# A second row added at the end of its own slot, sample heads picked two ahead, token rows in two buffers: an expert mixer beside dense steps

## Chip, cores and metric

One core of a Trainium2 chip. The time is that of one launch on the device in microseconds; lower is better. The median of three runs counts.

## What is computed

One layer of a streaming encoder for 1024 prompt tokens and 64 sample tokens: a dense part (input projection, three attention branches, gates, output projection), then for each token a mixture of single-neuron experts. Cut to the part that the change touches:

```python
def one_block(xb):                                   # 128 tokens, 8 heads
    q = (xb @ w_q).reshape(blk, PEER_HEADS, 2, PEER_DHALF)
    s = jnp.einsum('thpc,hpkc->thpk', q, sub_keys)
    s1, i1 = lax.top_k(s[:, :, 0], PEER_TOPK)        # 16 of 128 on each side
    s2, i2 = lax.top_k(s[:, :, 1], PEER_TOPK)
    ...
    top, pos = lax.top_k(cand, PEER_TOPK)            # 16 of the 256 sums
    idx = jnp.take_along_axis(cidx, pos, axis=-1)
    g = jax.nn.softmax(top, axis=-1)
    u = jnp.take(u_tab, idx, axis=0)
    a = jax.nn.gelu(jnp.einsum('thkd,td->thk', u, xb), approximate=False)
    w = (g * a).astype(xb.dtype)
    return jnp.einsum('thk,thkd->td', w, jnp.take(v_tab, idx, axis=0))
```

Every token fetches 8 x 16 rows of u and v by its own numbers: 128 tokens of a tile fetch one row of 8 KB (u and v side by side) in one gather.

## The kernel before

**Tiles and groups.** The tokens are 9 tiles (8 of 128, and the sample tile of 64). They form four groups: tile 0; 1 and 2; 3 to 5; 6 to 8. While the expert work of a group runs, the dense steps of the next group run beside it. The dense steps of a group are preparation and input projection (in_prep, in_unit), attention (mix, fox, past), gates (gate), output projection (out) and the scores of the experts (sco).

**Pairs and slots.** The expert work of a head is cut into pairs of two expert ranks: 8 pairs a head, 4 in the sample tile, where two halves of 64 partitions share a gather. `make_plan` lays out one slot for each pair and spreads the dense steps over the slots of a group by their given costs, so that they are done 16 slots before the group's end. The last 16 slots of each of the first three groups, and all 160 slots of the last group, have no dense step. Every engine walks through this plan in the same order (`walk`, L657), each with its own part. VectorE, ScalarE and GpSimd take the pair first and the dense steps of the slot after it; TensorE and SP take the dense steps first.

**A pair.** GpSimd issues two indirect gathers into a ring of 8 rows, that is 4 pairs (`gather`, L1798, the issue on L1814), three pairs ahead. VectorE multiplies the u half of each row with the token rows `h_cur` and sums (`dot`, L1726, the instruction on L1733). ScalarE waits for that, takes the Gelu (L1414), multiplies it with the softmax weight (L1417) and writes the weight onto a diagonal (L1422). TensorE multiplies the diagonal with the v half into the sum `p_y` (L1250).

**The second row.** In tiles 0 to 5 TensorE takes only the first row of a pair. The second is added by VectorE (`values`, L1738, the instruction on L1749): weight times v half plus `ysb`. VectorE does this for pair n-1 behind the dot products of pair n. It waits for `s_diag` (ScalarE has made the weights) and raises `s_vapart`. GpSimd gathers pair n only when TensorE is done with pair n-4 (`s_vdone`) and, in these tiles, VectorE has added its second row.

**The pick.** VectorE finds the 16 experts of a head in four pieces (`pick`, L1762): best of each side; best sums, first and second half; expert numbers and softmax weights. It does the pieces for head n+1 in the slots q = 0 to 3 of head n, behind dot products and addition. `softmax_weights` (L1713) writes numbers and weights into one of two buffers. In a prompt head the last four slots have no piece. In a sample head all four slots have one, and the numbers are ready at the head's end. ScalarE's exponentials for it (`soften`, L1403) stand behind the weights of q = 2.

**The token rows.** `h_cur` is one buffer. SP waits for the last dot product of tile i and then loads the rows of tile i+1 (`load_h`, L903, issued on L906, called from L926 ff.). The scores of head n+2 are loaded at the first slot of head n (`load_sc`, L896), behind the store of the tile before where a tile begins.

```python
        def pair(i, r, q):                       # VectorE, L1780
            dot(i, r, q)
            values(pair_index(i, r, q) - 1)
            if r == 0 and q == 0 and i:
                finish(i - 1)
            pick(i * HEADS + r + 1, q)
```

Of the kernel before, what the change touches and what calls it, by code (L numbers as in the profile page):

```python
# [71 lines left out]
def pairs_of(i):  # L72
    return 8 if i < TILES else 4
# [15 lines left out]

ALL_PAIRS = [(i, r, q) for i in range(NT) for r in range(HEADS) for q in range(pairs_of(i))]  # L90
ALL_HEADS = [(i, r) for i in range(NT) for r in range(HEADS)]


def weight_items():
# [369 lines left out]
def layer(nc, c, t_in, outs, dram, ctx):  # L464
# [76 lines left out]


    ring = c.ring
    h_cur = sb("h_cur", [128, D])
    diag = sb("diag", [128, RING, 128])
    sc = [sb(f"sc{k}", [128, 256]) for k in range(2)]
    v16 = sb("v16", [128, 2, TOPK])
# [9 lines left out]
    isel = sb("isel", [128, 2, TOPK])  # L557
    smx = sb("smx", [128, 4])
    ex = sb("ex", [128, TOPK])
    idx = sb("idx", [128, 2, TOPK], U32)  # L560
    gw = sb("gw", [128, 2, TOPK])
    dots = sb("dots", [128, TOPK])
    gel = sb("gel", [128, TOPK])
    wgt = sb("wgt", [128, TOPK])
# [89 lines left out]
    def k_store(t):  # L654
        return s_kTput[t % 2], 16 * (t // 2 + 1)

    def walk(front, experts, front_first):  # L657

        for expert, beside in PLAN:
            if not front_first and expert and expert[0] in experts:  # L660
                experts[expert[0]](*expert[1:])
            for step in beside:
                if step[0] in front:
                    front[step[0]](*step[1:])
            if front_first and expert and expert[0] in experts:
                experts[expert[0]](*expert[1:])


    @block.sync
    def _(sp):  # L670
# [231 lines left out]

        def load_h(i):  # L903
            T = width_of(i)
            sp.wait_ge(s_spill[i % 2], 32 * (i // 2 + 1))
            sp.dma_start(h_cur[:T, :], h_sp[rows(i), :]).then_inc(s_hcur, 16)  # L906
            if i == TILES:
                sp.dma_start(h_cur[T:2 * T, :], h_sp[rows(i), :]).then_inc(s_hcur, 16)

        def load_x1(i):  # L910
            if i >= 2:
# [14 lines left out]
        def pair(i, r, q):  # L926
            n = i * HEADS + r
            if q == 0:
                if r == 0 and i:
                    store_y(i - 1)  # L930
                if n + 2 < len(ALL_HEADS):
                    sp.wait_ge(s_sfree, n + 1)
                    load_sc(n + 2)
                if r == HEADS - 1 and i + 1 < NT:
                    load_x1(i + 1)
            if r == HEADS - 1 and q == pairs_of(i) - 1 and i + 1 < NT:
                sp.wait_ge(s_dot, pair_index(i, r, q) + 1)
                load_h(i + 1)

        def end():  # L940
            store_y(NT - 1)
# [318 lines left out]
    def _(act):  # L1260
# [147 lines left out]
        def weigh(i, r, q):  # L1408
            n, head = pair_index(i, r, q), i * HEADS + r
            T, unit = (128, c.ident) if i < TILES else (SAMPLE_T, c.fold)  # L1410
            c0 = q * PAIR
            act.wait_ge(s_dot, n + 1)
            n_e = 2 * n
            a_(gel[:, c0:c0 + PAIR], dots[:, c0:c0 + PAIR], ACT.Gelu).then_inc(s_ae, 1)  # L1414
            act.wait_ge(s_ae, n_e + 1)
            for k in range(PAIR):
                ins = nc.scalar.mul(wgt[:, c0 + k:c0 + k + 1], gel[:, c0 + k:c0 + k + 1],  # L1417
                                    gw[:, head % 2, c0 + k:c0 + k + 1])
            ins.then_inc(s_ae, 1)
            act.wait_ge(s_ae, n_e + 2)  # L1420
            for k in range(1 if apart(n) else PAIR):
                ins = nc.scalar.mul(diag[:, (n * PAIR + k) % RING, :T], unit[:, :T], wgt[:, c0 + k:c0 + k + 1])  # L1422
            ins.then_inc(s_diag, 1)
# [4 lines left out]
        def pair(i, r, q):  # L1428
            n = i * HEADS + r
            if q == 0:  # L1430
                act.wait_ge(s_idx, n + 1)
                if i == TILES:
                    link(nc.scalar.copy(gw[SAMPLE_T:128, n % 2, 0:8], gw[0:SAMPLE_T, n % 2, 8:16]))
            weigh(i, r, q)
            if q == 2 and n + 1 < len(ALL_HEADS):
                soften(n + 1)

        walk({"in_prep": in_prep, "in_unit": in_unit_, "mix": mix, "fox": fox,
              "past": past, "gate": gate, "out": out_, "sco": sco_}, {"start": start, "pair": pair}, False)
# [3 lines left out]
    def _(dve):  # L1443
# [269 lines left out]
        def softmax_weights(n):  # L1713
            i, r = ALL_HEADS[n]
            T = width_of(i)
            if n:

                dve.wait_ge(s_diag, pair_index(*ALL_HEADS[n - 1], 0))
            nc.vector.scalar_tensor_tensor(out=idx[:T, n % 2, :], in0=isel[:T, 0, :], scalar=float(NK),
                                           in1=isel[:T, 1, :], op0=ALU.mult, op1=ALU.add)  # L1720
            dve.wait_ge(s_ex, n + 1)
            linked(nc.vector.reciprocal(smx[:T, 2:3], smx[:T, 1:2]))
            nc.vector.tensor_scalar(out=gw[:T, n % 2, :], in0=ex[:T, :], scalar1=smx[:T, 2:3], scalar2=None,
                                    op0=ALU.mult).then_inc(s_idx, 1)

        def dot(i, r, q):  # L1726
            n = pair_index(i, r, q)
            if r == 0 and q == 0:
                dve.wait_ge(s_hcur, 16 * (i + 1 if i < TILES else TILES + 2))
            for k in range(PAIR):  # L1730
                j, turn = (n * PAIR + k) % RING, (n * PAIR + k) // RING
                dve.wait_ge(s_slot[j], 16 * (turn + 1))
                ins = nc.vector.tensor_tensor_reduce(  # L1733
                    out=ring[:, j, 0:D], in0=ring[:, j, 0:D], in1=h_cur[:, :], scale=1.0, scalar=0.0, op0=ALU.mult,
                    op1=ALU.add, accum_out=dots[:, q * PAIR + k:q * PAIR + k + 1])
            ins.then_inc(s_dot, 1)

        def values(n):  # L1738
            if n < 0 or not apart(n):
                return  # L1740
            i, r, q = ALL_PAIRS[n]
            T, j, col = width_of(i), (n * PAIR + 1) % RING, q * PAIR + 1
            if r == 0 and q == 0:
                dve.wait_ge(s_xres, 16 * (i + 1))
            if n:
                dve.wait_ge(s_vapart, apart_before(n))
            dve.wait_ge(s_diag, n + 1)
            y = ysb[i % 2]
            nc.vector.scalar_tensor_tensor(out=y[:T, :], in0=ring[:T, j, D:2 * D], scalar=wgt[:T, col:col + 1],  # L1749
                                           in1=y[:T, :], op0=ALU.mult, op1=ALU.add).then_inc(s_vapart, 1)  # L1750
# [9 lines left out]
            tt(out=y[:T, :], in0=p_y[:T, :], in1=y[:T, :], op=ALU.add).then_inc(s_yev, 1)  # L1760

        def pick(n, piece):  # L1762
            if n >= len(ALL_HEADS):
                return
            if piece == 0:
                best_of_side(n, 0)
                best_of_side(n, 1)
            elif piece == 1:
                best_sums_first(n)
            elif piece == 2:  # L1770
                best_sums_second(n)
            elif piece == 3:
                expert_numbers(n)
                softmax_weights(n)
# [4 lines left out]

        def pair(i, r, q):  # L1780
            dot(i, r, q)
            values(pair_index(i, r, q) - 1)
            if r == 0 and q == 0 and i:
                finish(i - 1)
            pick(i * HEADS + r + 1, q)

        def end():
            finish(NT - 1)

        walk({"in_prep": in_prep, "in_unit": in_unit_, "mix": mix, "fox": fox,  # L1790
              "past": past, "gate": gate, "out": out_, "sco": sco_}, {"start": start, "pair": pair, "end": end}, False)


    @block.gpsimd
    def _(pool):
        n_copied = [0]

        def gather(n):  # L1798
            i, r, q = ALL_PAIRS[n]
            head = i * HEADS + r  # L1800
            if q == 0:
                pool.wait_ge(s_idx, head + 1)
                if i == TILES:
                    n_copied[0] += 1
                    pool.tensor_copy(idx[SAMPLE_T:128, head % 2, 0:8], idx[0:SAMPLE_T, head % 2, 8:16])\
                        .then_inc(s_idx2, 1)
                    pool.wait_ge(s_idx2, n_copied[0])
            if n >= RING // PAIR:
                pool.wait_ge(s_vdone, n - RING // PAIR + 1)
                if apart(n - RING // PAIR):  # L1810
                    pool.wait_ge(s_vapart, apart_before(n - RING // PAIR + 1))
            for k in range(PAIR):
                j, col = (n * PAIR + k) % RING, q * PAIR + k
                nc.gpsimd.indirect_dma_start(  # L1814
                    out=ring[:, j, :], out_offset=None, in_=t_in["uv"][:, :],
                    in_offset=bass.IndirectOffsetOnAxis(ap=idx[:, head % 2, col:col + 1], axis=0)
                ).then_inc(s_slot[j], 16)

        LEAD = RING // PAIR - 1

        def start():
            for n in range(LEAD):
                gather(n)

        def pair(i, r, q):
            n = pair_index(i, r, q) + LEAD
            if n < len(ALL_PAIRS):
                gather(n)

        walk({}, {"start": start, "pair": pair}, False)  # L1830
# [82 lines left out]
```

## Time and profile before

| | us |
|---|---|
| median of three runs | 4593.27 |
| lowest and highest | 4581.66, 4601.18 |
| the profiled execution | 4590.58 |
| span of the profiled execution | 4588.9 |
| busy: TensorE matmul | 3432.5 (75%) |
| busy: VectorE | 2800.5 (61%) |
| busy: ScalarE | 1582.8 (34%) |
| busy: GpSimd | 1189.3 (26%) |
| gathers' share of 16 DMA engines' span | 63.3% |

The profile names engines PE (TensorE matmul), PEld (its weight loads), DVE (VectorE), ACT (ScalarE), POOL (GpSimd) and SP (SyncE); a q behind a name is the engine's queue. Times count from the span's start. An arrow "out<-in" names what an instruction writes and reads; behind a bar stand the idle time before it and what ended that. The shares of busy time are means over stretches with different limits, so the stretches are told apart: pairs of tile 0 run from about 420 to 1117, of tiles 1 and 2 to 2256, of tiles 3 to 5 to 3691, of tiles 6 and 7 to 4351; the sample tile runs to the end.

### The profile page before, as it was taken

What the parts mean: (1) busy time and instruction counts of PE and PEld (TensorE: products, weight loads), DVE (VectorE), ACT (ScalarE), POOL (GpSimd) and SP (SyncE); (2) the same over time, 40 slices, a digit from 0 to 9 for tenths busy, and PEclk for the clock granted to TensorE, in tenths of its full rate; (3) what the DMA queues carried; (4) which work ended last, traced back from release to release, by engine and by line L of the source; (5) the groups of instructions that cost most, each with busy time, mean ns of one, the idle gap of its engine ahead of it and who ended that gap; (6) DMA issues with size and microseconds to landing.
All of it is one profiled execution on the core that took longest, in us unless ns stands there. A gap on an engine that the chain in (4) does not pass through costs nothing.

```text
span 4588.9 us, 33986 instructions
## 1 busy us (share of the span) xinstructions
PE 3432.5 (75%) x10219; PEld 1773.8 (39%) x10219; DVE 2800.5 (61%) x6048; ACT 1582.8 (34%) x3680; POOL 1189.3 (26%) x1122
## 2 busy tenths in 40 slices
PE   5775866995987769989598666658888767777755
PEld 4462445841444434544143444325443222223211
DVE  1113464548566756555876887756666876766665
ACT  1211253423225544432322554424432223333322
POOL 0001111113221212222333222232223444444422
PEclk8887977997987779999699777779989889999988
DMA  7467856889976787789999889788989999999966
GB/s 245 170 233 271 317 192 224 319 332 382 354 306 243 278 301 290 296 320 360 372 420 386 314 302 325 246 335 323 360 320 386 384 403 421 421 411 420 407 273 281
DMA packets 298493, 1484.95 MB, mean 324 GB/s; under 512 B 42741, under 2 KB 112373, under 8 KB 147717
## 3 DMA queue, kind: packets, MB, share of 16 engines
q0 software_dynamic: 156672, 1140.92, 63.3%
q1 hardware_dynamic: 141636, 341.86, 20.4%
q8 instruction: 81, 1.33, 0.1%
q14 instruction: 104, 0.84, 0.0%
HBM read 1415.59 MB, written 67.08 MB: 323 GB/s over the span
## 4 chain that ended last, share of the span: by engine, by line
PE 45%; DMA 18%; DVE 17%; issue 8%; ACT 7%; POOL 2%; SPq 1%; POOLq 0%; DVEq 0%; ACTq 0%
PE c_p_y L1250 12%; DMA c_ring<-in_uv,l_idx 11%; DVE c_ring L1733 7%; PE c_PB L982 4%; PE c_PC L982 4%; PE c_PA L1192 3%; PE c_PB L1237 3%; PE c_PA L1237 3%; PE c_PB L1192 2%; PE c_PC L1192 2%; DVE l_ysb L1749 2%; POOL c_ring L1814 2%; DMA c_area<-oT_sp 2%; PE c_PA L1220 2%; PE c_PB L1195 1%
## 5 line engine op out<-in xcount | busy, mean ns | idle before, releaser
L1814 POOL DMA_INDIRECT c_ring<-in_uv,l_idx x1088 | 1182.8, 1087 | 3245.8 <-DVE l_ysb L1749 1943.2
L1250 PE MATMUL c_p_y<-c_ring,l_diag 128*128 128x512 f32 (+1 forms) x2816 | 1551.1, 691 | 570.5 <-ACT l_diag L1422 553.6
L1733 DVE CUSTOM_DVE_ANT_0 c_ring<-c_ring,l_h_cur 128x1024 f32<-128x1024 f32 x1088 | 1298.5, 1220 | 373.3 <-DMA c_ring<-in_uv,l_idx 319.4
L1250 PEld LDWEIGHTS c_p_y<-c_ring,l_diag 128*128 128x128 f32 (+1 forms) x2816 | 556.5, 209 | 1379.5 <-ACT l_diag L1422 764.1
L1414 ACT ACTIVATE l_gel<-l_dots 128x2 f32<-128x2 f32 x544 | 110.7, 204 | 1608.4 <-DVE l_dots L1733 1607.1
L1749 DVE SCALAR_TENSOR_TENSOR l_ysb<-c_ring,l_wgt,l_ysb 128x1024 f32<-128x1024 f32 x384 | 491.7, 1281 | 1.0 <-ACT l_diag L1422 1.0
L1414 ACT ACT_TABLE_LOAD x208 | 266.9, 1283 | 50.1 <-DVE l_dots L1733 46.7
L1417 ACT ACTIVATE l_wgt<-l_gel,l_gw 128x1 f32<-128x1 f32 x1088 | 261.2, 287 | 17.8
L1422 ACT ACTIVATE l_diag<-c_ident,l_wgt 128x128 f32<-128x128 f32 x640 | 242.9, 398 | 16.7
L982 PE MATMUL c_PB<-c_area 128*128 128x451 f32 (+1 forms) x576 | 226.1, 546 | 2.8 <-DMA c_area<-in_w_in 2.8
L982 PE MATMUL c_PC<-c_area 128*128 128x451 f32 (+1 forms) x576 | 224.4, 542 | 3.8 <-DMA c_area<-in_w_in 3.8
L1192 PE MATMUL c_PA<-c_area 128*128 128x128 f32 (+3 forms) x512 | 135.5, 422 | 114.9 <-DMA c_area<-oT_sp 112.8
L1633 DVE TENSOR_TENSOR c_area<-c_area,c_PA 128x128 f32<-128x128 f32 (+3 forms) x32 | 14.0, 437 | 235.2 <-ACT c_area L1371 235.2
L1192 PEld LDWEIGHTS c_PA<-c_area 128*128 128x128 f32 x512 | 96.1, 208 | 158.5 <-issue 130.3
L982 PEld LDWEIGHTS c_PB<-c_area 128*128 128x128 f32 (+1 forms) x576 | 106.3, 186 | 122.1 <-issue 117.6
L982 PEld LDWEIGHTS c_PC<-c_area 128*128 128x128 f32 (+1 forms) x576 | 105.1, 183 | 121.1 <-issue 114.9
L1132 PE MATMUL c_PC<-c_ident,c_area 128*128 128x128 f32 (+2 forms) x328 | 67.8, 323 | 99.1 <-ACT c_area L1358 55.1
L1237 PE MATMUL c_PA<-c_area 128*128 128x512 f32 (+1 forms) x288 | 130.3, 607 | 1.9 <-ACT c_area L1380 1.9
L1237 PE MATMUL c_PB<-c_area 128*128 128x512 f32 (+1 forms) x288 | 128.3, 599 | 2.6 <-DMA c_area<-rw_sp 2.6
L1192 PE MATMUL c_PC<-c_area 128*128 128x128 f32 (+3 forms) x512 | 126.8, 402 | 0.0
L1192 PE MATMUL c_PB<-c_area 128*128 128x128 f32 (+3 forms) x512 | 123.8, 395 | 0.0
L1132 PEld LDWEIGHTS c_PC<-c_ident,c_area 128*128 128x128 f32 (+2 forms) x328 | 45.2, 167 | 161.1 <-ACT c_area L1358 74.1
(284 smaller groups left out, 3728.9 us busy)
## 6 DMA issues: line engine op xcount, KB each, us to landing
c_area<-in_w_gb SPq DMA_DIRECT2D x32, 2304.0 KB, 11.6
c_area<-in_w_in SPq DMA_DIRECT2D x32, 1804.0 KB, 9.3
c_area<-rw_sp SPq DMA_DIRECT2D x16, 2048.0 KB, 10.3
c_ring<-in_uv,l_idx POOLq DMA_INDIRECT x1088, 9.4
c_area<-in_w_out SPq DMA_DIRECT2D x8, 2048.0 KB, 10.4
proj<-c_area SPq DMA_DIRECT2D x64, 225.5 KB, 7.7
c_area<-proj SPq DMA_DIRECT2D x8, 1288.0 KB, 5.8
c_ring<-in_w_qT SPq DMA_DIRECT2D x16, 512.0 KB, 7.5
```

The lines of the kernel that those rows point to most:

```text
L982: ins = mm_(banks[2 + u % 4][:T, :PW], hT_in[:, dt, j * 128:j * 128 + T], w[:, dt * PW:(dt + 1) * PW], start=dt == 0, stop=dt == DT - 1)
L1132: ins = tr_(PC[:widths[b], (b % 4) * 128:(b % 4) * 128 + T], prob[h % 2][:T, b * 128:b * 128 + widths[b]], c.ident[:T, :T])
L1192: mm_(ps[:, 0:N], w[:, at:at + 128], g_hT[:, e, 0:N], start=e == 0, stop=e == DT - 1)
L1220: ins = mm_((PA, PB)[j % 2][:T, half * 512:(half + 1) * 512], mixT[:, dt, j * 128:j * 128 + T], w[:, dt * 512:(dt + 1) * 512], start=dt == ...
L1237: ins = mm_(banks[v % 4][:T, :], hT_out[:, dt, j * 128:j * 128 + T], w[:, dt * 512:(dt + 1) * 512], start=dt == 0, stop=dt == DT - 1)
L1250: ins = mm_(p_y[:T, e * 512:(e + 1) * 512], diag[:, j, :T], ring[:, j, D + e * 512:D + (e + 1) * 512], start=r == 0 and q == 0 and k == 0, ...
L1414: a_(gel[:, c0:c0 + PAIR], dots[:, c0:c0 + PAIR], ACT.Gelu).then_inc(s_ae, 1)
L1417: ins = nc.scalar.mul(wgt[:, c0 + k:c0 + k + 1], gel[:, c0 + k:c0 + k + 1], gw[:, head % 2, c0 + k:c0 + k + 1])
L1422: ins = nc.scalar.mul(diag[:, (n * PAIR + k) % RING, :T], unit[:, :T], wgt[:, c0 + k:c0 + k + 1])
L1733: ins = nc.vector.tensor_tensor_reduce(out=ring[:, j, 0:D], in0=ring[:, j, 0:D], in1=h_cur[:, :], scale=1.0, scalar=0.0, op0=ALU.mult, op1 ...
L1749: nc.vector.scalar_tensor_tensor(out=y[:T, :], in0=ring[:T, j, D:2 * D], scalar=wgt[:T, col:col + 1], in1=y[:T, :], op0=ALU.mult, op1=ALU. ...
L1814: nc.gpsimd.indirect_dma_start(out=ring[:, j, :], out_offset=None, in_=t_in["uv"][:, :], in_offset=bass.IndirectOffsetOnAxis(ap=idx[:, hea ...
```

## The change

VectorE's addition of the second row moves from behind the next pair's dot products to the end of the pair's own slot, behind its dense steps (`walk` gets a fourth argument that is called there). The sample heads are picked two heads ahead: head 63 picks heads 64 and 65, in its slots 0 to 3 and 4 to 7, and sample head n picks n+2; numbers and weights get a third buffer for it, ScalarE's exponentials follow the same order. The token rows get a second buffer, and their load goes to the first slot of a tile's last head, behind a wait for the dot products of the tile before (the buffer's last reader).

```diff
+def pick_at(i, r, q):
+    n = i * HEADS + r
+    if i == TILES:
+        n += 2
+    elif n == TILES * HEADS - 1:
+        n += 1 + q // 4
+    else:
+        n += 1
+        if q >= 4:
+            return None, None
+    return (n, q % 4) if n < len(ALL_HEADS) else (None, None)
...
-    h_cur = sb("h_cur", [128, D])
+    h_cur = [sb(f"h_cur{k}", [128, D]) for k in range(2)]
...
-    idx = sb("idx", [128, 2, TOPK], U32)
-    gw = sb("gw", [128, 2, TOPK])
+    idx = sb("idx", [128, 3, TOPK], U32)
+    gw = sb("gw", [128, 3, TOPK])
...
-    def walk(front, experts, front_first):
+    def walk(front, experts, front_first, late=None):
...
             if front_first and expert and expert[0] in experts:
                 experts[expert[0]](*expert[1:])
+            if late and expert and expert[0] == "pair":
+                late(pair_index(*expert[1:]))
...
         def load_h(i):
             T = width_of(i)
+            if i >= 2:
+                sp.wait_ge(s_dot, pair_index(i - 1, 0, 0))
             sp.wait_ge(s_spill[i % 2], 32 * (i // 2 + 1))
-            sp.dma_start(h_cur[:T, :], h_sp[rows(i), :]).then_inc(s_hcur, 16)
+            sp.dma_start(h_cur[i % 2][:T, :], h_sp[rows(i), :]).then_inc(s_hcur, 16)
...
                 if r == HEADS - 1 and i + 1 < NT:
                     load_x1(i + 1)
-            if r == HEADS - 1 and q == pairs_of(i) - 1 and i + 1 < NT:
-                sp.wait_ge(s_dot, pair_index(i, r, q) + 1)
-                load_h(i + 1)
+                    load_h(i + 1)
...
             weigh(i, r, q)
-            if q == 2 and n + 1 < len(ALL_HEADS):
-                soften(n + 1)
+            head, piece = pick_at(i, r, q)
+            if piece == 2:
+                soften(head)
...
-            if n:
-                dve.wait_ge(s_diag, pair_index(*ALL_HEADS[n - 1], 0))
-            nc.vector.scalar_tensor_tensor(out=idx[:T, n % 2, :], in0=isel[:T, 0, :], scalar=float(NK),
+            if n >= 3:
+                dve.wait_ge(s_diag, pair_index(*ALL_HEADS[n - 2], 0))
+            nc.vector.scalar_tensor_tensor(out=idx[:T, n % 3, :], in0=isel[:T, 0, :], scalar=float(NK),
                                            in1=isel[:T, 1, :], op0=ALU.mult, op1=ALU.add)
...
         def pair(i, r, q):
             dot(i, r, q)
-            values(pair_index(i, r, q) - 1)
             if r == 0 and q == 0 and i:
                 finish(i - 1)
-            pick(i * HEADS + r + 1, q)
+            pick(*pick_at(i, r, q))
...
         walk({"in_prep": in_prep, "in_unit": in_unit_, "mix": mix, "fox": fox,
-              "past": past, "gate": gate, "out": out_, "sco": sco_}, {"start": start, "pair": pair, "end": end}, False)
+              "past": past, "gate": gate, "out": out_, "sco": sco_}, {"start": start, "pair": pair, "end": end}, False, values)
```

The other lines of the diff turn `% 2` into `% 3` where numbers and weights are read, and `h_cur` into `h_cur[i % 2]`.

## Rows read from the trace of the kernel before

**Rows 1.** Stages: stretch, length, busy PE PEld DVE ACT POOL, clock, DMA share, GB/s.

```profile
1035.00:1117.00 82.00, 44.41 (x63) 13.74 (x61) 73.73 (x152) 23.31 (x72) 34.66 (x30) 0.77 0.99 387
2174.00:2256.00 82.00, 45.09 (x63) 14.09 (x61) 74.21 (x152) 23.29 (x72) 33.90 (x30) 0.75 1.00 400
2263.00:3610.00 1347.00, 1024.78 (x3063) 521.59 (x3064) 960.97 (x1973) 526.34 (x1150) 402.21 (x352) 0.86 0.88 338
3610.00:3691.00 81.00, 44.50 (x63) 14.82 (x61) 74.11 (x153) 23.26 (x72) 34.65 (x30) 0.76 0.98 393
3691.00:4351.00 660.00, 492.93 (x1020) 192.67 (x1020) 452.40 (x1092) 223.50 (x705) 278.79 (x258) 0.95 1.01 416
4351.00:4589.00 238.00, 137.47 (x264) 38.54 (x264) 139.03 (x382) 63.10 (x197) 64.00 (x67) 0.83 0.70 279
```

**Rows 2.** List of waits, 418 to 3698: us in total, times, longest us.

```profile
POOL c_ring L1814 <- DVE l_ysb L1749: 1935.1, 297, 45.5
...
PE c_p_y L1250 <- ACT l_diag L1422: 298.7, 116, 8.7
...
DVE c_ring L1733 <- DMA c_ring<-in_uv,l_idx: 61.8, 44, 6.1
```

**Rows 3.** List of waits, whole span.

```profile
DVE c_ring L1733 <- DMA l_h_cur<-h_sp: 46.4, 7, 10.4
```

**Rows 4.** List of waits, sample tile (4351 to the end).

```profile
POOL l_idx L1805 <- DVE l_gw L1723: 126.6, 7, 22.5
...
DVE c_ring L1733 <- DMA c_ring<-in_uv,l_idx: 76.9, 30, 6.5
```

**Rows 5.** Table by stages, one sample head.

```profile
4416.40:4445.20 28.80, 16.97 (x32) 4.72 (x32) 18.14 (x52) 8.24 (x25) 8.95 (x10) 0.81 0.73 293
```

**Rows 6.** Line L901, loads of scores, 3690 to the end.

```profile
DMA to landing us min/median/max: 3.7/6.9/9.8
```

**Rows 7.** Line L906, loads of token rows, whole span.

```profile
DMA to landing us min/median/max: 4.2/7.5/8.2
```

**Rows 8.** The page's costliest groups: busy, mean ns, idle before and releaser.

```profile
L1749 DVE SCALAR_TENSOR_TENSOR l_ysb<-c_ring,l_wgt,l_ysb 128x1024 f32<-128x1024 f32 x384 | 491.7, 1281 | 1.0 <-ACT l_diag L1422 1.0
```

**Rows 9.** Chain of waits in 418 to 3698, shares by line, then pieces: start, us.

```profile
by line: PE c_p_y L1250 12.2%; DVE c_ring L1733 7.9%; issue 6.8%; PE c_PB L982 5.4%; PE c_PC L982 5.2%; DMA c_ring<-in_uv,l_idx 3.9%; PE c_PA L1237 3.4%; PE c_PA L1192 3.3%; DVE l_ysb L1749 3.3%; PE c_PB L1237 3.2%; PE c_PB L1192 3.2%; PE c
...
612.02 1.22 DVE c_ring L1733
...
613.24 1.14 DVE c_ring L1733
...
3129.06 0.50 DVE c_area L1633
...
3132.74 0.41 ACT l_diag L1422
...
3133.20 2.96 PE c_p_y L1250 x4
...
3629.65 1.20 DVE l_ysb L1749
...
3633.36 1.22 DVE c_ring L1733
```

**Rows 10.** Timeline of pair 52: start us, us, engine, line, operation.

```profile
1060.12 0.07 DVE L1733 DVE_READ_ACCUMULATOR2_ANT l_dots<- 128x1 f32 x1
...
1060.23 0.20 ACT L1414 ACTIVATE l_gel<-l_dots 128x2 f32<-128x2 f32 x1 [4.97 <-DVE l_dots L1733]
...
1060.98 0.40 ACT L1422 ACTIVATE l_diag<-c_ident,l_wgt 128x128 f32<-128x128 f32 x1
```

**Rows 11.** Timeline, two gathers' issues beside VectorE's dot products.

```profile
1045.60 0.94 POOL L1814 DMA_INDIRECT c_ring<-in_uv,l_idx  x1 [4.40 <-DVE l_ysb L1749]
...
1046.71 1.22 DVE L1733 CUSTOM_DVE_ANT_0 c_ring<-c_ring,l_h_cur 128x1024 f32<-128x1024 f32 x1
...
1046.84 1.91 POOL L1814 DMA_INDIRECT c_ring<-in_uv,l_idx  x1 [0.30 <-issue]
```

More of the change, by code:

```diff
@@ L904, in load_h @@
             T = width_of(i)
+            if i >= 2:
+                sp.wait_ge(s_dot, pair_index(i - 1, 0, 0))
             sp.wait_ge(s_spill[i % 2], 32 * (i // 2 + 1))
-            sp.dma_start(h_cur[:T, :], h_sp[rows(i), :]).then_inc(s_hcur, 16)
+            sp.dma_start(h_cur[i % 2][:T, :], h_sp[rows(i), :]).then_inc(s_hcur, 16)
             if i == TILES:
-                sp.dma_start(h_cur[T:2 * T, :], h_sp[rows(i), :]).then_inc(s_hcur, 16)
+                sp.dma_start(h_cur[i % 2][T:2 * T, :], h_sp[rows(i), :]).then_inc(s_hcur, 16)
         def load_x1(i):
@@ L1417, in weigh @@
                 ins = nc.scalar.mul(wgt[:, c0 + k:c0 + k + 1], gel[:, c0 + k:c0 + k + 1],
-                                    gw[:, head % 2, c0 + k:c0 + k + 1])
+                                    gw[:, head % 3, c0 + k:c0 + k + 1])
             ins.then_inc(s_ae, 1)
@@ L1432, in pair @@
                 if i == TILES:
-                    link(nc.scalar.copy(gw[SAMPLE_T:128, n % 2, 0:8], gw[0:SAMPLE_T, n % 2, 8:16]))
+                    link(nc.scalar.copy(gw[SAMPLE_T:128, n % 3, 0:8], gw[0:SAMPLE_T, n % 3, 8:16]))
             weigh(i, r, q)
-            if q == 2 and n + 1 < len(ALL_HEADS):
-                soften(n + 1)
+            head, piece = pick_at(i, r, q)
+            if piece == 2:
+                soften(head)
         walk({"in_prep": in_prep, "in_unit": in_unit_, "mix": mix, "fox": fox,
@@ L1722, in softmax_weights @@
             linked(nc.vector.reciprocal(smx[:T, 2:3], smx[:T, 1:2]))
-            nc.vector.tensor_scalar(out=gw[:T, n % 2, :], in0=ex[:T, :], scalar1=smx[:T, 2:3], scalar2=None,
+            nc.vector.tensor_scalar(out=gw[:T, n % 3, :], in0=ex[:T, :], scalar1=smx[:T, 2:3], scalar2=None,
                                     op0=ALU.mult).then_inc(s_idx, 1)
@@ L1733, in dot @@
                 ins = nc.vector.tensor_tensor_reduce(
-                    out=ring[:, j, 0:D], in0=ring[:, j, 0:D], in1=h_cur[:, :], scale=1.0, scalar=0.0, op0=ALU.mult,
+                    out=ring[:, j, 0:D], in0=ring[:, j, 0:D], in1=h_cur[i % 2][:, :], scale=1.0, scalar=0.0, op0=ALU.mult,
                     op1=ALU.add, accum_out=dots[:, q * PAIR + k:q * PAIR + k + 1])
@@ L1738, in values @@
         def values(n):
-            if n < 0 or not apart(n):
+            if not apart(n):
                 return
@@ L1762, in pick @@
         def pick(n, piece):
-            if n >= len(ALL_HEADS):
-                return
             if piece == 0:
@@ L1804, in gather @@
                     n_copied[0] += 1
-                    pool.tensor_copy(idx[SAMPLE_T:128, head % 2, 0:8], idx[0:SAMPLE_T, head % 2, 8:16])\
+                    pool.tensor_copy(idx[SAMPLE_T:128, head % 3, 0:8], idx[0:SAMPLE_T, head % 3, 8:16])\
                         .then_inc(s_idx2, 1)
@@ L1815, in gather @@
                     out=ring[:, j, :], out_offset=None, in_=t_in["uv"][:, :],
-                    in_offset=bass.IndirectOffsetOnAxis(ap=idx[:, head % 2, col:col + 1], axis=0)
+                    in_offset=bass.IndirectOffsetOnAxis(ap=idx[:, head % 3, col:col + 1], axis=0)
                 ).then_inc(s_slot[j], 16)
```

## The prediction

> **What bounds the kernel now.** I read the page first, then the table by stages, the list of waits, the chain of waits, and timelines of single slots. The program has three kinds of stretch, and the table by stages keeps them apart [rows 1].
>
> The first kind is a stretch in which the next group's dense steps run beside the expert pairs; 2263 to 3610 us stands for it. Its DMA share is 0.88, TensorE is busy for 1025 of 1347 us, VectorE for 961: nobody is full, and the order of the work decides. The second kind is the tail of a group, 16 pairs without dense steps (1035, 2174 and 3610 us): DMA share 0.98 to 1.00 and 81 or 82 us each. The third is the last group. Tiles 6 and 7 (3691 to 4351) run at a DMA share of 1.01, so the gathers alone set their pace; the sample tile (4351 to the end) falls back to 0.70.
>
> The waits of the first three groups [rows 2] tell what not to count. GpSimd sits idle for 1935 us on the addition of the second row (L1749), but an idle GpSimd costs nothing unless the next dot product comes too early for its row, and VectorE waits only 61.8 us for gathered rows there. That is the whole prize for freeing slots earlier, not the 1935. TensorE waits 298.7 us for diagonals of weights. Over the whole span VectorE waits for token rows 7 times, 46.4 us in sum [rows 3]. In the sample tile GpSimd waits for expert numbers 7 times, 126.6 us in all, and VectorE then waits 76.9 us for rows [rows 4].
>
> **The sample tile, term by term.** Head n's numbers are ready only at the end of head n-1, so the gathers of a new head start with the ring drained. From 4351 to the end are 238 us; about 10 of them lie behind the last dot product (weights, matmul, add, store), so 32 pairs take 228 us. One head, 4416.4 to 4445.2, takes 28.8 us with 18.1 us of VectorE work [rows 5]. Picked two heads ahead, the numbers are there in time, and the pairs should run at the pace of tiles 6 and 7: 660 us, less their two token-row waits of about 7.5 each, over 128 pairs, is 5.04 us a pair, 161 us for 32. VectorE's 18.1 us for four pairs stay under 20.2, though not by much. Head 63 now picks two heads, the second in slots that were free. One load comes late: the scores of head 66 are asked for behind the store of tile 7 on SP, and VectorE's pick stands behind it; such a load takes 6.9 us at the median [rows 6]. So 168 us for 228: **-60**. The 10.4 us token-row wait of this tile is part of that. Bounds: -67 (no late load) and -40 (VectorE, not DMA, sets 22 us a head, and the load is late too).
>
> **Token rows in two buffers.** Today SP waits for a tile's last dot product and only then loads the next rows, 4.2 to 8.2 us to landing [rows 7]. Afterwards the load goes out seven pairs earlier, on SP ahead of the dense loads of seven slots, which it holds up by its issue alone. Six waits other than the sample's make 36 us. Part comes back by itself today, since the ring fills meanwhile, so I take three quarters: **-27**, between -15 and -40. The upper end is over 36 because SP also stands in that wait with the next group's first loads queued behind it, and now isn't. The wait added in its place, for the dots of the tile before the last, has long been met. It costs nothing: the load is covered by seven pairs, some 35 us. The third buffer of numbers and weights only turns a wait for one head back into one for two heads back, both long met.
>
> **The second row, moved in front of the next dot product.** The addition takes 1.28 us and practically never waits now (1.0 us over 384 of them [rows 8]). The number of instructions stays. What changes is who stands behind whom: before, VectorE goes dot n+1, add n, pick; ScalarE makes the weights of n+1 beside the add. After, it goes add n, dot n+1, so the weights of n+1, and TensorE's pair behind them, come 1.28 us later wherever VectorE enters the slot straight from a wait. [rows 9] shows such a place: the gate product ends at 3129.56, the dots follow at once, the diagonal ends at 3133.15, and only then TensorE goes on. On the chain of waits from 418 to 3698 I count 55 visits that come from VectorE's other work, take the dots and leave to ScalarE, the first at 612.0, the last at 3633.4 [rows 9]. 55 x 1.28 is **+70**. Visits that take dot and add in a row come out even. The least would be 20 visits: dot products are 7.9% of that stretch of the chain and adds 3.3%, or 259 us at 2.36 us a pair and 108 us at 1.20 (the durations of such pieces), 110 pairs against 90 adds; +26. The most is every TensorE wait, 116 times 1.28: +148, far too much where other engines bind.
>
> **The wait inside the slot.** Now the add of a slot needs weights of the same slot. Behind the dots of pair 52, which end at 1060.12, ScalarE takes until 1061.38 [rows 10]: 1.26 us in which a slot with neither pick nor dense VectorE work has nothing to do. The plan in the code has 79 such slots, 24 of them in the three tails. A tail now has about 75 us of VectorE occupancy in 82 (the rest is mostly the row waits); 8 x 1.2 more gives 84.7, so +2.7 a tail, **+8**. Of the other 55, most stand beside gate or projection matmuls that last 6 us and more, which hide it; I take one in seven, **+10**, between 0 and 55 x 1.26 = +69.
>
> **Slots freed earlier.** The gather of pair n+4 no longer stands behind dot n+1: 2.4 us earlier, in the tails less, since TensorE's pair then frees the slot last. On the chain nine visits leave to the gather; 9 x 2.4 and a little more is **-25**, between 0 and the 61.8 us of [rows 2].
>
> Against this part speaks an observation. A gather issued at 1045.60 takes 0.94 us on GpSimd; the next, under the two dots, 1.91 [rows 11]. Freed by the add, more gathers will meet the dots right behind it. The Trainium skill, SBUF — State Buffer, section "Who interferes with whom", says that a VectorE instruction with two SBUF inputs contends with a GpSimd instruction that reads SBUF, whichever comes second being held until the first ends; these rows agree in direction, and by that rule the term would be near 0. I keep -25, since about 1 us is short against the 2.4 us won.
>
> **Sum.** -60 -27 +70 +8 +10 -25 = -24. The profiled execution took 4590.6 us (span 4588.9), 2.7 under the median of 4593.3; the forecast is 4567 us, taken against the former. What a measurement of this kernel can tell from no change is about 0.5%, 23 us: under 4570 is faster, over 4616 slower. So the forecast lies close to that border.
>
> **The rivals.**
> - *The move costs little* (0.25). The 55 visits and the stalls fall mostly where gathers or another engine have slack; then only sample, token rows and ring remain with some 25 of loss: -87, 4504 us. For it: the DMA share of 0.88, which says that a later TensorE is partly absorbed. Against it: TensorE stands right behind the diagonal in [rows 9], with its next matmuls following without a gap.
> - *The wait inside the slot decides* (0.20), the side of slower. Place: slots of the first three groups without pick and dense VectorE work, and dense steps that only ScalarE evicts. Price 1.26 us each time, plus the 1.28 that shifts dot n+1. If all 55 pay rather than one in seven (+59) and half of the ring's gain is eaten (+13): 4639 us. It decides once more than about 50 of these 79 slots have no cover. For it: that the add never waits today says only that it stands one slot late. Against it: the 6 us matmuls beside most of them.
> - *The gathers meet the dots* (0.12), by [rows 11]. The freed slots are worth nothing, sum +1: 4592 us, no change. Against it: the shortest gather that waits for a row still has 5 us a pair, of which two issues take under 3.
> - *The sample's head start does not arrive* (0.05): scores land late in every head, not only for head 66, 6.9 us each; 7 x 6.9 of the 60 is lost: 4615 us, just no change. Against it: SP has nothing between these loads in the last group.
>
> **How the numbers follow.** The forecast has 0.38, on its own 4535 to 4600. Half of it and the first rival lie under 4570: faster 0.45. The other half, the gathers and the sample rival give no change, 0.33. The wait inside the slot, with a little of the rest, gives slower 0.22. Leaving out about 0.1 on either side, the range is 4500 to 4640.
>
> **What would show it.** Right: the sample tile with a DMA share near 1 and about 170 us long; GpSimd's wait for numbers gone but for the start; no wait of VectorE for token rows; TensorE's wait for diagonals in 418 to 3698 up by 50 to 90 us; L1749's line with a wait on ScalarE of 30 to 80 us where it had 1.0; VectorE's wait for rows well under 61.8. The forecast is wrong if TensorE's wait for diagonals stays as it was while the total falls by more than 70 us, if the sample tile stays above 200 us, or if the first three groups together grow by more than 80 us.

## The result and the profile after

The changed kernel takes 4622.33 us (median of four runs, 4612.99 to 4624.16), the kernel before, run beside it, 4587.47 us. The ratio is 1.007, with a 95% interval of 1.0052 to 1.0087: 35 us slower, where the forecast was 24 us faster. The profiled execution has a span of 4621.1 us.

The table by stages, in the stretches that answer to [rows 1] (length, busy PE PEld DVE ACT POOL, clock, DMA share, GB/s): the three tails, the body of tiles 3 to 5, tiles 6 and 7, the sample.

```profile
1039.00:1118.00 79.00, 44.99 (x56) 13.95 (x56) 69.02 (x145) 21.12 (x64) 32.45 (x28) 0.72 1.01 409
2200.00:2280.00 80.00, 43.04 (x57) 13.75 (x56) 69.92 (x147) 21.72 (x67) 32.63 (x29) 0.74 1.01 412
2287.00:3696.00 1409.00, 1051.86 (x3068) 534.23 (x3066) 961.37 (x1973) 526.09 (x1150) 399.18 (x352) 0.84 0.85 323
3696.00:3775.00 79.00, 42.79 (x56) 13.75 (x56) 69.21 (x146) 21.80 (x67) 35.44 (x29) 0.74 0.99 392
3782.00:4434.00 652.00, 480.87 (x1011) 187.30 (x1009) 454.53 (x1116) 222.11 (x699) 275.26 (x254) 0.97 1.01 415
4434.00:4621.00 187.00, 127.64 (x272) 36.40 (x272) 135.70 (x357) 64.52 (x202) 69.53 (x68) 0.95 0.89 361
```

The sample tile went from 238 to 187 us and its DMA share from 0.70 to 0.89: that part worked. The tails did not grow. The body of tiles 3 to 5 did: 1409 us where it had 1347, with VectorE busy for the same 961 us. So nothing was added to VectorE there; things stand in another order. TensorE, with as many matmuls as before (3068 and 3063), was busy for 27 us more, at a granted clock of 0.84 where it was 0.86 [rows 1]; the other 35 us are idle time of TensorE.

To compare stretches exactly I take them from the first dot product of one pair to that of another, out of the traces (us). The "bodies" are the first three groups without their tails; next_all is an experiment below, the change with its adds left behind the next dot products:

| | before | after | next_all |
|---|---|---|---|
| three bodies | 3012.7 | 3104.2 | 3000.0 |
| three tails | 266.3 | 259.1 | 259.2 |
| tiles 6 and 7 | 662.3 | 658.6 | 661.5 |
| sample, to the end | 228.8 | 181.0 | 181.9 |

The list of waits of after from 418 to 3782, as [rows 2] (us in total, times, longest):

```profile
PE c_p_y L1267 <- ACT l_diag L1439: 356.7, 131, 8.6
...
DVE l_ysb L1767 <- ACT l_diag L1439: 119.5, 95, 3.8
...
DVE c_ring L1751 <- DMA c_ring<-in_uv,l_idx: 9.5, 5, 6.2
```

VectorE's waits for gathered rows are down from 61.8 us to 9.5, which was the aim, and the stretch is 84 us longer all the same. In their place stand 119.5 us in which the add waits for its own weights, and TensorE waits 58 us more for diagonals. The chain of waits of the same stretch shows where the time went (first line: shares by line; [rows 9] has it of before):

```profile
by line: PE c_p_y L1267 12.2%; DVE c_ring L1751 11.9%; DVE l_ysb L1767 6.6%; PE c_PB L999 5.5%; PE c_PC L999 5.1%; issue 4.9%; PE c_PA L1209 3.3%; PE c_PB L1209 3.2%; PE c_PA L1254 3.1%; PE c_PB L1254 3.1%; PE c_PC L1209 3.1%; DMA c_area<-o
```

Dot products and adds have 18.5% of the chain where they had 11.2%. The adds alone stand on it 177 times instead of 90. Sorted by the plan, most of the growth lies in the slots in which VectorE has a dense step: 123 adds on the chain, before 54; in all other slots together 54, before 36.

One such place is the gate product of [rows 9]. In the kernel before, the add stood behind the two dot products that follow it, beside ScalarE's work on their weights (start us, us, engine, line, operation):

```profile
3131.88 1.28 DVE L1749 SCALAR_TENSOR_TENSOR l_ysb<-c_ring,l_wgt,l_ysb 128x1024 f32<-128x1024 f32 x1
```

The same place in the timeline of after:

```profile
3180.39 0.49 DVE L1651 TENSOR_TENSOR c_area<-c_area,c_PA 128x320 f32<-128x320 f32 x1 [3.55 <-ACT c_area L1388]
...
3180.92 1.28 DVE L1767 SCALAR_TENSOR_TENSOR l_ysb<-c_ring,l_wgt,l_ysb 128x1024 f32<-128x1024 f32 x1
...
3182.12 1.22 DVE L1751 CUSTOM_DVE_ANT_0 c_ring<-c_ring,l_h_cur 128x1024 f32<-128x1024 f32 x1
...
3185.27 0.40 ACT L1439 ACTIVATE l_diag<-c_ident,l_wgt 128x128 f32<-128x128 f32 x1
...
3185.73 3.55 PE L1267 MATMUL c_p_y<-c_ring,l_diag 128*128 128x512 f32 x4 [4.12 <-ACT l_diag L1439]
```

VectorE waited 3.55 us for ScalarE, in both kernels. Now the add stands behind that wait, between the gate product and the dot products, and pushes them back: from the gate product's start to TensorE's matmul it is 5.34 us, where it was 4.14 [rows 9].

### The profile page after: what moved, and what is told of

Its sections match the earlier page's. It is cut to its first block, busy times and chain, and to the rows that moved or that the text cites. A ratio compares the mean times of both kernels' runs of the same rounds, so it can differ in the third digit from the quotient of the medians.

```text
span 4621.1 us, 33857 instructions
## 1 busy us (share of the span) xinstructions
PE 3454.1 (75%) x10219; PEld 1783.0 (39%) x10219; DVE 2802.9 (61%) x6048; ACT 1582.3 (34%) x3680; POOL 1207.7 (26%) x1122
## 4 chain that ended last, share of the span: by engine, by line
PE 45%; DVE 22%; DMA 17%; ACT 8%; issue 4%; POOL 1%; SPq 1%; DVEq 0%; POOLq 0%; ACTq 0%
PE c_p_y L1267 13%; DMA c_ring<-in_uv,l_idx 10%; DVE c_ring L1751 10%; DVE l_ysb L1767 5%; PE c_PB L999 4%; PE c_PC L999 4%; PE c_PA L1209 3%; PE c_PA L1254 3%; PE c_PB L1209 3%; PE c_PC L1209 2%; PE c_PB L1254 2%; DMA c_area<-oT_sp 2%; ACT l_wgt L1434 2%; ACT l_diag L1439 2%; PE c_PA L1237 1%
## 5 line engine op out<-in xcount | busy, mean ns | idle before, releaser
L1829 POOL DMA_INDIRECT c_ring<-in_uv,l_idx x1088 | 1200.8, 1104 | 3389.9 <-PE c_p_y L1267 1572.4
L1767 DVE SCALAR_TENSOR_TENSOR l_ysb<-c_ring,l_wgt,l_ysb 128x1024 f32<-128x1024 f32 x384 | 491.9, 1281 | 124.4 <-ACT l_diag L1439 119.5
```

Source lines behind the costliest of these rows:

```text
L1829: nc.gpsimd.indirect_dma_start(out=ring[:, j, :], out_offset=None, in_=t_in["uv"][:, :], in_offset=bass.IndirectOffsetOnAxis(ap=idx[:, hea ...
```

## Experiments

Theory D: an add behind a dense VectorE step holds up the next dot products, their weights and TensorE's pair by its own length. Theory W: the loss is the wait for weights in slots with nothing else to do. Theory SP: the earlier load of token rows holds up the dense loads on SP. Later ones (F, O, N, E and H) are named in the expectations of their runs. Unless it is said otherwise a diff is against the changed kernel. The ratio is to the kernel before, run beside each batch, with medians from 4583.8 to 4590.2 us.

| kernel | median us | ratio to before | 95% interval |
|---|---|---|---|
| next_all | 4525.21 | 0.9864 | 0.9847 to 0.9881 |
| move_only | 4700.04 | 1.0236 | 1.0220 to 1.0252 |
| own_dense | 4605.52 | 1.0044 | 1.0029 to 1.0058 |
| own_rest | 4534.70 | 0.9882 | 0.9865 to 0.9899 |
| own_early | 4522.59 | 0.9853 | 0.9832 to 0.9875 |
| half_next | 4484.90 | 0.9774 | 0.9754 to 0.9794 |
| half_dense | 4532.95 | 0.9877 | 0.9858 to 0.9896 |
| sample_only | 4538.48 | 0.9892 | 0.9871 to 0.9913 |
| rows_only | 4574.90 | 0.9983 | 0.9970 to 0.9996 |
| next_ring6 | 4835.74 | 1.0535 | 1.0513 to 1.0556 |
| after_ring6 | 4801.83 | 1.0466 | 1.0445 to 1.0488 |
| early_ring6 | 4791.47 | 1.0443 | 1.0423 to 1.0462 |

**The move taken back, and the move alone.** next_all puts the add behind the next dot products again and keeps the rest:

```diff
         def pair(i, r, q):
             dot(i, r, q)
+            if pair_index(i, r, q):
+                values(pair_index(i, r, q) - 1)
...
-              ... "end": end}, False, values)
+              ... "end": end}, False)
```

move_only does the opposite to the kernel before (with the changed `walk`):

```diff
             dot(i, r, q)
-            values(pair_index(i, r, q) - 1)
...
-              ... "end": end}, False)
+              ... "end": end}, False, values)
```

> The changed kernel with the add put back behind the next dot products; sample heads and token rows stay as changed. Theory D (the add, put behind the dense VectorE step, holds up the next dot products): the groups return to the time before, the sample keeps its 48 us, token rows some 8: 4531 us. Theory W (the wait inside slots without other work costs): the same 4531. Theory SP (the token-row load in a tile's last head holds up SP's dense loads): the groups stay long, 4590 to 4615.

> The kernel before with nothing changed but the place of the add. D and W: the groups grow by 84 to 92 us, all else stays: 4672 to 4680 us. SP: the move costs little, 4585 to 4600.

Measured 4525.2 and 4700.0. The move is the whole loss, and SP is not in it: without the move the change is a gain of 1.4%. By medians the move costs 97 us on top of the other parts; alone it costs 110, more than the 84 to 92 that either theory gave. In the profiled executions the bodies grow by the same 104 us both times (to 3116.6 in move_only); the difference lies outside them, more than half of it in the tails, 274.8 in move_only against 266.3 before, where after and next_all have the same 259. Why the tails differ was not tried.

**Which slots.** Only the slots with a dense VectorE step (228 of 384), or only the other 156, keep the add at the end of their own slot; `on_vector` says whether VectorE has a part in a dense step:

```diff
+        def own_slot(n):
...
+            beside = BESIDE[n]
+            return any(map(on_vector, beside))
...
+            n = pair_index(i, r, q)
             dot(i, r, q)
+            if n and not own_slot(n - 1):
+                values(n - 1)
...
+        def behind_dense(n):
+            if own_slot(n):
+                values(n)
...
-              ... "end": end}, False, values)
+              ... "end": end}, False, behind_dense)
```

In own_rest the condition is `not any(map(on_vector, beside))`.

> The changed kernel, but only in the 228 slots of tiles 0 to 5 in which VectorE has a dense step is the add at the end of its own slot; in the other 156 it is behind the next dot products. D: nearly all of the loss stays, 4605 to 4625 us. W: the loss is gone with the 79 waits, 4525 to 4545.

> The reverse: the add at the end of its own slot in the 156 slots without a dense VectorE step, behind the next dot products in the 228 with one. D: the loss is gone, 4510 to 4540 us, under the version with no move at all if slots freed earlier are worth something. W: the 79 waits of 1.35 us stay, 107 us in sum as in the changed kernel, and the loss with them: 4600 to 4620.

own_dense has 4605.5, 80 us over next_all; own_rest has 4534.7, 9.5 over it, with intervals that just overlap. D holds and W falls. The waits of next_all, own_dense and own_rest, from 418 to the end of tile 5 in each (3678, 3760, 3698); ahead of the first two stands the stretch itself, as in [rows 1]:

```profile
418.00:3678.00 3260.00, 2530.05 (x7596) 1349.28 (x7596) 2139.86 (x4405) 1230.86 (x2650) 838.15 (x769) 0.86 0.84 323
...
PE c_p_y L1267 <- ACT l_diag L1439: 302.7, 113, 7.4
...
DVE c_ring L1751 <- DMA c_ring<-in_uv,l_idx: 73.5, 53, 6.1
```

```profile
418.00:3760.00 3342.00, 2561.50 (x7597) 1361.08 (x7598) 2139.02 (x4406) 1228.85 (x2652) 898.28 (x768) 0.85 0.83 315
...
PE c_p_y L1284 <- ACT l_diag L1456: 351.7, 122, 8.6
...
DVE c_ring L1768 <- DMA c_ring<-in_uv,l_idx: 55.3, 36, 6.1
...
DVE l_ysb L1784 <- ACT l_diag L1456: 15.2, 15, 4.1
```

```profile
PE c_p_y L1284 <- ACT l_diag L1456: 311.1, 120, 7.4
...
DVE l_ysb L1784 <- ACT l_diag L1456: 58.0, 41, 3.8
...
DVE c_ring L1768 <- DMA c_ring<-in_uv,l_idx: 24.3, 15, 6.3
```

own_dense hardly makes the add wait and loses 80 us; TensorE's wait for diagonals grows by 49. In own_rest one VectorE wait took the place of another: rows fell by 49 us, weights rose by 57 (from 1.4), and TensorE's wait rose by 8. Only 41 adds wait there, where W had 79; so the rest is also taken from the other side: after, with all 79 waits, has 17 us over own_dense. The adds of the rest cost 9 to 17 us by medians (20 in this stretch of own_rest, which is 3280 us long), those of the dense slots 80 to 88. On the chain, 121 adds of dense slots in own_dense stand against 55 in next_all; 66 more at 1.28 us is 84 us, near the 80 measured. The 80 us are also 63 of 228 adds at full price: about one dense slot in four pays.

Not all of the price is waiting. The stretch of own_dense is 82 us longer than that of next_all; TensorE is idle for 51 of these and busy for 31 more, with the same matmuls at a lower granted clock (0.85 and 0.86). What the clock would have been without the longer waits was not tried.

**Is it the length?** half_next has the order of next_all, half_dense that of own_dense. In both the adds take only the first 512 of 1024 columns; the other half of the second row is left out:

```diff
-            nc.vector.scalar_tensor_tensor(out=y[:T, :], in0=ring[:T, j, D:2 * D], ...
-                                           in1=y[:T, :], ...
+            nc.vector.scalar_tensor_tensor(out=y[:T, 0:512], in0=ring[:T, j, D:D + 512], ...
+                                           in1=y[:T, 0:512], ...
```

> All adds behind the next dot products, and each adds only the first 512 of 1024 columns (the second row's other half is left out). The base for the next run: some 4470 to 4500 us, since 88 adds stand on the chain of waits and each gets about 0.6 us shorter.

> The same half adds (512 of 1024 columns, the rest left out), in the 228 slots with a dense VectorE step at the end of the own slot. D: the loss goes with the length of the add, 40 to 45 us over the run with half adds behind the next dot products, where whole adds lost 80. Rival O (the order itself costs, a wait or a missed start per slot whatever the length): 70 to 90 us over it.

4484.9 and 4533.0: 48 us apart. The line of the page for the add in half_dense:

```profile
L1784 DVE SCALAR_TENSOR_TENSOR l_ysb<-c_ring,l_wgt,l_ysb 128x512 f32<-128x512 f32 x384 | 286.7, 747 | 19.8 <-ACT l_diag L1456 17.1
```

A half add takes 747 ns, 0.58 of 1281; 0.58 of 80 us is 47. That is a little over the 40 to 45 that D gave and far under the 70 to 90 of O: the loss goes with the length of the add, and not with the order as such.

**The same add, ahead of the dense step.** own_early adds in the own slot too, but between pick and dense step, in the 192 slots that have a piece of the pick:

```diff
+            n = pair_index(i, r, q)
             dot(i, r, q)
+            if n and ALL_PAIRS[n - 1][2] >= 4:
+                values(n - 1)
...
             pick(*pick_at(i, r, q))
+            if q < 4:
+                values(n)
...
-              ... "end": end}, False, values)
+              ... "end": end}, False)
```

> Sample heads and token rows as changed; in the slots with a piece of the pick the add comes at its own slot too, but right behind that piece and ahead of the dense step; in the others behind the next dot products. D (only an add between a dense step and the next dot products costs): no loss, 4505 to 4530 us against 4525 with all adds behind the next dot products, the lower end if rows freed earlier shorten VectorE's 73.5 us of waits for rows. Rival F (any add in its own slot costs, since gathers then start at other times and meet dots and dense loads): a good part of the loss is back, 4560 to 4605.

4522.6 us: no loss, and no gain over next_all that the intervals would show. F falls. The run covers about half of D's case: of the 192 slots 115 have a dense VectorE step, and 60 of the 121 adds on the chain of own_dense stand in these, so behind the step they would have cost some 40 us (an estimate, half of 80). The 113 dense slots without a piece of the pick were not tried with the add ahead. The gathers' issue in own_early, then in next_all (the page's groups):

```profile
L1834 POOL DMA_INDIRECT c_ring<-in_uv,l_idx x1088 | 1232.6, 1133 | 3254.0 <-PE c_p_y L1267 1704.9
```

```profile
L1831 POOL DMA_INDIRECT c_ring<-in_uv,l_idx x1088 | 1185.0, 1089 | 3306.7 <-DVE l_ysb L1767 1916.2
```

An issue takes 44 ns longer, 48 us over all gathers, and the total isn't longer for it.

**The other two parts.** sample_only is the kernel before with `pick_at` and the third buffers alone; rows_only is the kernel before with two `h_cur` and the early `load_h` alone. Cut to the core, against the kernel before:

```diff
             if r == 0 and q == 0 and i:
                 finish(i - 1)
-            pick(i * HEADS + r + 1, q)
+            pick(*pick_at(i, r, q))
```

```diff
-    h_cur = sb("h_cur", [128, D])
+    h_cur = [sb(f"h_cur{k}", [128, D]) for k in range(2)]
...
                     load_x1(i + 1)
-            if r == HEADS - 1 and q == pairs_of(i) - 1 and i + 1 < NT:
-                sp.wait_ge(s_dot, pair_index(i, r, q) + 1)
-                load_h(i + 1)
+                    load_h(i + 1)
```

> The kernel before with the sample heads picked two ahead, and nothing else. If the sample's head start is worth what its stretch shows (228.8 to 181 us from its first dot product to the end): 4538 to 4545 us, and the token rows in two buffers then hold the 15 to 20 us down to 4525. If the token rows do nothing outside the sample: 4525 to 4530.

> The kernel before with the token rows in two buffers, and nothing else. By the other runs (the sample alone 4538, with the rows 4525): 13 to 20 us, 4570 to 4577. By the term of the prediction, 27 us: 4563.

The sample alone is worth 52 us, the rows in two buffers 13 behind it and 8 by themselves (ratio 0.9983, interval 0.9970 to 0.9996, so 2 to 14). The 13 are no firmer, since the intervals of sample_only and next_all overlap.

**What are earlier rows worth?** With 8 rows in the ring nothing was seen of it. So the ring was cut to 6, in next_all, in the changed kernel and in own_early.

```diff
-RING = 8
+RING = 6
```

> All adds behind the next dot products, sample and token rows as changed, and a ring of 6 rows instead of 8, so that each gather stands behind the pair three back. Both theories: clearly longer than 4525, some 4600 to 4800 us. It is the base of the next run.

> The changed kernel, the add at the end of its own slot, with a ring of 6 rows. Theory N (rows freed earlier are worth nothing here, only the shift of the dot products counts): 85 to 110 us over the run with the add behind the next dot products and 6 rows, as with 8. Theory E (rows freed earlier are worth something as soon as the ring is short; with 8 rows it was not): under 60 us over it, or even below it.

> A ring of 6 rows, and the add right behind its own pick and ahead of the dense step in the slots that have a piece of the pick, behind the next dot products in the others. With 6 rows the changed order won 34 us where with 8 it lost 97, a swing of 131. Theory E (rows freed earlier are what was won, and the loss is the dense step's alone): these 192 slots free their rows early and delay nothing, so about half of the 131 is won, 4755 to 4785 us, under both other runs with 6 rows. Theory H (the win comes from the slots without a pick, q of 4 to 7, where this order changes nothing): 4815 to 4840, as with the add behind the next dot products.

Now the changed order is 34 us faster than the old one, where with 8 rows it was 97 slower. The first three groups of next_ring6 (418 to 3846) and of after_ring6 (418 to 3814), table by stages and waits:

```profile
418.00:3846.00 3428.00, 2588.51 (x7596) 1371.76 (x7596) 2149.98 (x4403) 1232.12 (x2648) 817.86 (x766) 0.84 0.82 307
...
DVE c_ring L1751 <- DMA c_ring<-in_uv,l_idx: 346.5, 216, 6.3
```

```profile
418.00:3814.00 3396.00, 2590.00 (x7596) 1373.08 (x7596) 2145.26 (x4404) 1229.75 (x2648) 842.68 (x767) 0.84 0.82 310
...
DVE l_ysb L1767 <- ACT l_diag L1439: 121.0, 94, 5.0
...
DVE c_ring L1751 <- DMA c_ring<-in_uv,l_idx: 54.3, 45, 6.2
```

VectorE's waits for rows are 346.5 us with the old order and 54.3 with the new one; 292 us of waits are gone, 121 us of waits for weights have come, and these groups are 32 us shorter. E holds, N falls. By the traces nearly all of it lies in the tails, where no dense step stands: 310.0 us with the old order and 281.4 with the new; in the bodies, 3119.2 and 3115.7, gain and price are about even. early_ring6, at 4791.5, gains 44 us on next_ring6 without the dense step's price. That is a third of the swing of 131 where E expected about half, and between the ranges of E and H: neither was met. That the rest of the swing lies in the last four slots of a head is likely, but no run has it apart. That early_ring6 lies 10 us below after_ring6 is within the intervals.

## Why the prediction was wrong, and where it was right

By its own terms, predicted and measured:

| term | predicted | measured | from |
|---|---|---|---|
| sample | -60 | -52 | sample_only, which keeps its token-row wait |
| token rows | -27 | -13 | next_all less sample_only |
| the move, all four terms | +63 | +97 | after less next_all |
| sum | -24 | +32 | after, beside its own before: +35 |

**The sample** came nearly as worked out: GpSimd's 126.6 us of waits for numbers [rows 4] are gone from the list, and a pair takes 5.1 us in the steady part (two heads, 8 pairs, in 40.6 and 40.7 us between first dot products). The -60 counted the tile's own token-row wait as gone, and sample_only keeps 7.7 us of it; taken together, sample and rows were to give 87 us and gave 65 (next_all). The prediction's lower bound of -40 is -45 by its own numbers (8 heads of 22 us and a load of 6.9 for 228). The one late load of scores is there, 10.1 us where 6.9 was taken:

```profile
DVE l_v L1693 <- DMA l_sc<-sc_sp: 10.1, 1, 10.1
```

**Token rows**: VectorE's waits for them, 46.4 us [rows 3], are all gone, but only 13 of the 27 us arrived. "Three quarters" was too much: of the 36 us outside the sample about a third was won. That the ring fills during such a wait would explain it, but isn't shown.

**The dot products moved back** were the right mechanism at about the right size: +70 forecast, 80 measured in own_dense, with whatever the ring gave back in these slots (VectorE's waits for rows fell there from 73.5 to 55.3 us). The count of 55 chain visits was a little low: 80 us are 63 adds. That TensorE's matmuls would also run longer was in no term.

**The wait inside the slot** was named as the rival on the side of slower, and its time, 4639, is near 4622; but it isn't the cause; that the number is near is luck. The waits did come, 119.5 us in 95 slots, all 79 among them, beyond the 30 to 80 that the text wanted to see. They cost little: own_rest, which has 58 us of them, pays 9.5 in all, and in after the adds of these slots cost 17 on top of own_dense. The +8 of the tails isn't shown: after has 7.5 us more there than own_dense (259.1 and 251.6), but no more than next_all (259.2).

**"Slots freed earlier", -25**, is the step that failed. The waits for rows fell by 52 us and no gain shows. In the slots without a dense step the wait for weights took their place (own_rest: -49 and +57); and in own_early, where the add stands ahead of the dense step and waits 25.6 us in all, they fall by 12 us and the total by 3, inside the intervals. I took the row waits for time to be won. With 8 rows other waits took their place. With 6 rows, where they are 346.5 us, the same edit wins. The runs give only gain and price together for each kind of slot, so that the gain is nil is a reading of these waits and of own_early, not a measurement by itself.

So the sum missed by 56 us: 34 in the move (25 of them the ring's term, the rest the higher count and what the two kinds of slots cost together, 97 against 80 + 9.5), 14 in the token rows, 8 in the sample. The ring's term is the largest, but without it the forecast would have been +1, still not +35. The text's own mark of being wrong, that the first three groups grow by more than 80 us, was met: 84. Of its marks of being right, three on waits were met as well (no wait for token rows, 58 us more for diagonals, 9.5 us for rows): a wait that goes isn't yet time that is won.

**The gathers meet the dots**: by [rows 11] and the rule of the Trainium skill (SBUF — State Buffer, "Who interferes with whom") issues under the dot products should get longer. The rule says that a VectorE instruction with two SBUF inputs and a GpSimd instruction that reads SBUF hold each other up, and the one that comes second waits. Whether the issue of a gather counts as such an instruction no run here shows. In the trace of the kernel before, the 242 issues that meet no VectorE instruction take 938 ns in the mean, the 364 that lie mostly under a dot product 1291: this agrees in direction. But the total doesn't follow it. The mean issue of all gathers is 1087 ns in the kernel before, 1104 in after, 1133 in own_early, 1142 in own_rest and 1148 in own_dense; after, which lost most, has the least of it, and own_early lost no time.

The best versions are next_all and own_early, 1.4 and 1.5% under the kernel before and not to be told apart: the sample and the token rows as changed, and the add behind the next dot products, or behind its own pick and ahead of the dense step.

## What to carry to other kernels

On an engine that runs in order, filler work belongs in front of an instruction that waits for others, not behind it: there it is done in the wait (own_early, 4522.6 us), behind it part of it goes to whoever waits for the next result (own_dense, 4605.5). A wait in the list is a prize only if nothing else would end at the same moment; before an edit is made for it, ask which wait comes next, and test by making the resource scarcer, as the ring of 6 rows did: the same edit lost 97 us with 8 rows and won 34 with 6.

## What was not expected of the hardware

An add of half the columns takes more than half the time: 747 to 749 ns for 128x512 and 1279 to 1285 for 128x1024, so by an estimate from these two lengths about 0.22 us do not depend on the columns (2 x 748 - 1281 = 215 ns). And the ring's size has a price of its own that the place of the adds can't change: tiles 6 and 7, where VectorE adds no second row, take 661.5 us with 8 rows and 781.1 with 6 (next_all, next_ring6), 786.1 with the changed order.
